# Seven more dummy products per layer on TensorE, in the pauses of the routing chain of a hybrid attention and mixture-of-experts backbone

## The reference, cut to what matters

```python
p_grp = softmax(h @ w_rg + b_rg)            # 4 groups
p_top, g_idx = top_k(p_grp, 1)              # one group
e_in = (h @ w_re + b_re)[group g_idx]       # 8 experts in it
l_top, e_loc = top_k(e_in, 2)               # two experts
w_tok = p_top * softmax(l_top)
...                                         # tokens sorted by expert, in blocks of 128 rows
yb = (silu(xblk @ w_gate[e]) * (xblk @ w_up[e])) @ w_down[e]
out = zeros.at[row_tok].add(yb * row_w)
```

## Time and profile before

| what | us |
|---|---|
| median of 3 executions (2642.61 to 2646.21) | 2644.64 |
| the profiled execution, whole | 2650.5 |
| its span from first to last instruction | 2648.7 |
| TensorE busy in it | 2452.0 (93%) |
| VectorE, ScalarE, GpSimd busy | 944.8, 662.6, 352.6 |

### The profile page before, as it was taken

One profiled execution on the slowest core, in us unless ns is written; L12 is line 12 of the kernel. 1 busy time (PEld: TensorE's weight loads), 2 busy tenths in 40 slices (PEclk: granted clock), 3 DMA queues, 4 the chain that ended last, 5 costly groups with the idle time before them and its releaser, 6 DMA issues.

```text
span 2648.7 us, 32996 instructions
## 1 busy us (share of the span) xinstructions
PE 2452.0 (93%) x12867; PEld 1556.2 (59%) x12867; DVE 944.8 (36%) x1791; ACT 662.6 (25%) x1242; POOL 352.6 (13%) x404
## 2 busy tenths in 40 slices
PE   7999999999999798999996999999999988999995
PEld 4768666788888633443332668667888733343332
DVE  3335466622225730000003635566334731111113
ACT  3231445632222200110111521456333200000000
POOL 1241000000112220010001531000011220010002
PEclk9999999999999889999998999999999889999998
DMA  8671001322214599999998471004433799999995
GB/s 283 205 269 49 7 1 45 78 61 70 64 56 167 216 387 422 427 422 425 427 427 326 165 245 48 7 1 98 113 96 109 294 374 424 427 421 424 427 427 198
DMA packets 218636, 604.66 MB, mean 228 GB/s; under 512 B 63360, under 2 KB 139552, under 8 KB 184944
## 3 DMA queue, kind: packets, MB, share of 16 engines
q1 hardware_dynamic: 190514, 526.80, 52.1%
q0 software_dynamic: 24512, 63.13, 6.8%
q10 hardware_dynamic: 3456, 12.58, 1.2%
HBM read 585.96 MB, written 38.16 MB: 236 GB/s over the span
## 4 chain that ended last, share of the span: by engine, by line
PE 71%; DMA 14%; DVE 7%; ACT 3%; issue 2%; SPq 1%; POOL 1%; DVEq 0%; ACTq 0%; POOLq 0%
PE slot L1239 23%; PE abank L778 18%; PE vbank L778 10%; DMA arena<-in_w_down_e 6%; DMA arena<-in_w_up_e 5%; PE slot L961 2%; PE vbank L995 1%; PE abank L878 1%; PE vbank L942 1%; DMA arena<-in_w_in 1%; PE slot L1022 1%; PE vbank L768 1%; PE slot L706 1%; PE vbank L1055 1%; DMA arena<-in_w_ada 1%
## 5 line engine op out<-in xcount | busy, mean ns | idle before, releaser
L1239 PE MATMUL slot<-arena 128*64 128x512 f32 (+2 forms) x3232 | 817.4, 613 | 66.6 <-DMA arena<-in_w_up_e 39.9
L1239 PEld LDWEIGHTS slot<-arena 128*64 128x64 f32 (+2 forms) x3232 | 296.1, 146 | 535.0 <-issue 527.2
L778 PE MATMUL abank<-round,round 128*128 128x512 f32 (+1 forms) x1792 | 492.7, 355 | 7.2 <-ACT arena L2275 2.1
L778 PEld LDWEIGHTS abank<-round,round 128*128 128x128 f32 x1792 | 318.7, 189 | 71.2 <-issue 15.9
L778 PE MATMUL abank<-hT_low,round 128*128 128x512 f32 (+1 forms) x896 | 318.1, 355 | 0.0
L778 PE MATMUL vbank<-round,round 128*128 128x512 f32 (+3 forms) x1248 | 289.9, 361 | 6.9 <-issue 5.8
L2110 DVE TENSOR_TENSOR arena<-slot,arena 128x512 f32<-128x512 f32 x76 | 52.6, 692 | 652.8 <-ACT arena L2515 378.8
L778 PEld LDWEIGHTS vbank<-round,round 128*128 128x128 f32 x1248 | 215.2, 189 | 41.8 <-issue 9.2
L778 PEld LDWEIGHTS abank<-hT_low,round 128*128 128x128 f32 x896 | 168.7, 188 | 23.9 <-issue 0.5
L1818 DVE TENSOR_TENSOR arena<-vbank,arena 128x512 f32<-128x512 f32 x72 | 43.4, 602 | 291.9 <-PE vbank L778 284.3
L2692 POOL TENSOR_TENSOR arena<-arena 128x512 f32<-128x512 f32 (+1 forms) x48 | 55.9, 1164 | 578.5 <-DVE arena L1818 578.5
(11 more groups left out here) (337 smaller groups left out, 2882.4 us busy)
## 6 DMA issues: line engine op xcount, KB each, us to landing
arena<-in_w_down_e SPq DMA_DIRECT2D x44, 2048.0 KB, 22.8
arena<-in_w_gate_e SPq DMA_DIRECT2D x40, 2048.0 KB, 25.0
arena<-in_w_up_e SPq DMA_DIRECT2D x40, 2048.0 KB, 29.8
arena<-in_w_up_e SPq DMA_DIRECT2D x48, 1024.0 KB, 13.0
arena<-in_w_gate_e SPq DMA_DIRECT2D x44, 1024.0 KB, 12.5
arena<-in_w_ada POOLq DMA_DIRECT2D x80, 512.0 KB, 4.9
arena<-in_w_down_e SPq DMA_DIRECT2D x40, 1024.0 KB, 29.9
arena<-in_w_in SPq DMA_DIRECT2D x48, 512.0 KB, 4.2
```

The lines of the kernel that those rows point to most:

```text
L778: last = pe.matmul(to, x, y, start=(k == 0 and q == 0), stop=(k == len(terms) - 1 and q == 2))
L1239: last = pe.matmul(to[at, cols], x[:, at], w[:, at_w, :], start=first, stop=final)
```

## The change

In each layer one dummy is added ahead of the router of the last tile, one after it, two ahead of the placement products, and three ahead of the first gathered rows. These are seven in each layer and fourteen in all. Nothing else changes; a line is added, so that lines of the new kernel from 1173 on stand one higher.

```diff
                     elif n == len(qt) - 1:
-                        keep_clock(spare, 1)
+                        keep_clock(spare, 2)
                     router(n)
-                keep_clock(spare, 2)
+                keep_clock(spare, 3)
 
                 pe.wait_ge(route_v, 3 * L + 1)
...
                 close(last, vgroups)
 
+                keep_clock(slot[0], 2)
                 ps = vec()
                 for k in range(2):
                     pe.wait_ge(route_p, 4 * L + k + 1)
...
-                keep_clock(slot[0], 2)
+                keep_clock(slot[0], 5)
                 xt_done, at_done = {}, {}
```

## The result

The changed kernel takes 2656.21 us (median of 17 executions, 2648.40 to 2661.72) against 2646.21 us for the kernel before (17 executions, 2642.22 to 2650.31). The ratio is 1.0036, with a 95% interval of 1.0029 to 1.0044: about 10 us slower. The forecast was 2645.5 us, range 2641.2 to 2650.0. The profiled execution after took 2659.0 us with a span of 2657.2 us, 8.5 us longer than that of before.

The account below looks back on a forecast made before the run. The prediction took the routing chain to bound the kernel until the weight stream takes over. Its terms, -1.2 us in layer 0 and +2.1 in layer 1, made +0.9, giving 2645.5 us from 2644.64, range 2641.2 to 2650.0.

Parts of the forecast that it names:

- What counts is what of it lies in a pause: Pricing step: fourteen dummies cost 12.0 us at full clock, 24.1 at half, but only work not hidden in pauses counts.
- B: Rival: the five dummies at the first rows run at half clock throughout, 8.6 us; 2650.4 us, chance 0.09.
- C: Rival: five dummies end in time, but the clock falls again during the rows' transposes and copies; 2649.9 us, chance 0.06.
- The row that the prediction set against C: Layer 1 before: the clock came back at 2135.3, right behind eight transposes of the first rows.
- The sum without this term: Net of all priced parts: -1.2 us in layer 0 and +2.1 in layer 1, together +0.9 us.
- One more ahead of the last router: Added dummy delays the last router's transposes, with no pause to hide it: +1.2 us layer 0, +0.9 layer 1.
- One more behind it: Three dummies after the last router run at full clock, hidden by VectorE's choosing: 0.1 us for both layers.
- rank and placement products wait for VectorE as before: Sign of a right forecast: dummies behind the last router and at the placement stay hidden, delaying neither product group.
- Two at the placement: Two dummies ahead of the placement products end before the second group may start: 0, at most 0.2 us.
- Five at the rows: Five dummies ahead of the first rows start at half clock, take 6.4 to 7.4 us: +0.6 layer 0, +2.0 layer 1.
- What comes back: Full clock behind the five dummies speeds rows' transposes and layer 0's first experts: 3.1 us layer 0, 0.9 layer 1.
- The test on the last router: Sign of a right forecast: the last router's transposes start about 1.6 us later against VectorE's line 1894.

Follow-up runs that it names:

- experiment 1: Kernel before with no dummy added but 56 idle semaphore increments in layer 1's expert phase: 2652.38 us, ratio 1.0026.
- experiment 2: Changed kernel with all fourteen dummies plus 200 idle increments, moving layer 1's loop by 256 in all: 2647.89 us, ratio 1.0000 against the kernel before.
- experiment 10: Changed kernel, no fillers, with TensorE's loop over spare expert blocks skipped by a condition: 2648.43 us, ratio 1.0010 against the kernel before.
- experiment 4: Kernel before with five dummies in place of two ahead of the first rows, plus 232 idle increments: 2646.70 us, ratio 1.0012.
- experiment 3: Kernel before with 256 idle increments in layer 1's expert phase and nothing else: 2646.24 us, ratio 1.0004.
- experiment 9: Kernel before with TensorE's loop over spare expert blocks skipped by a condition: 2646.05 us, ratio 1.0003.
- experiment 11: Kernel before with 28 idle increments in layer 1's expert phase and nothing else: 2653.42 us in one execution.
- experiment 12: Kernel before with 84 idle increments in layer 1's expert phase and nothing else: 2647.52 us in one execution.

## Why the prediction was wrong

**The step that failed** is the sentence on which the sum was built, "What counts is what of it lies in a pause." It takes it that an added instruction costs only where it runs. The prediction priced fourteen dummies in their pauses. Nowhere did it ask what the 56 instructions move behind them. The missing term is about +7 us: experiment 1 measures +6.8 us (+4.2 to +9.3), and the profile shows 5.75 us of it between the last experts and the mixing product. The loop's place makes up about 7 of the 10 us; the other 3 have no cause shown, and experiments 2 and 10 leave 2.3 and 3.0 us by their medians, with intervals that hold zero. No rival had this mechanism either, and B and C, whose times came nearest, had another cause: the five did not run at half throughout (experiment 4 and the profile after), and the clock was full at the first expert products of both layers. The row that the prediction set against C settles less than it says, as 3.78 us of dummies ran ahead of those eight transposes.

**The sum without this term** was +0.9 us (+0.8 before its parts are rounded), and experiment 2 measures 0.0 (-2.4 to +2.6). Point by point:

- *One more ahead of the last router, +2.1 us.* The profile after has the pair at 2.69 us against 1.49 in layer 0, and 3.33 against 1.82 in layer 1, where the transposes behind it win back 0.5 us (1.41 against 1.91). That is 1.2 and 1.0 us more, near the 1.2 and 0.9 forecast. In layer 0 that is luck in part: the pair was the shorter for running partly at full clock, and the transposes won nothing back (1.67 against 1.72), where the forecast had 1.7 for the dummy and 0.45 back. (By its own times, a start at 916.2 and the clock back at 916.8, it should have had three transposes at half and about 0.6 back.) Alone its time can't be told from nothing.
- *One more behind it, 0.1 us.* Mis-sized as an argument: "the router in front of them has just run at full clock" does not keep the clock up. The rank products were late by 1.6 us in both layers of the profile after, and in seven of ten layers over all traces with the three dummies, so the sign "rank and placement products wait for VectorE as before" failed for the rank products. The other bound that the prediction named, half clock and 2.4 us late, has as much right as the one taken. The lateness does not show in the time of experiment 2.
- *Two at the placement, 0.* Right: full clock, hidden, and the dummy behind them at 1.10 us instead of 2.05.
- *Five at the rows, 6.4 to 7.4 us long.* Right, 6.58 and 6.91 us. Layer 1 is late by 2 to 3 us against the +2.0 taken.
- *What comes back, 3.1 and 0.9 us.* Against the one profile before, the durations came back as forecast: 0.60 for 1.12, and 3.65 for 5.81. But that was one execution: in five of ten cases of experiments 1, 3, 9, 11 and 12 the first experts ran at full clock without any added dummy. Five dummies gave full clock in all eight cases (the profile after, experiments 2, 4 and 10), so they make sure of what otherwise came in half of the cases, and the 3.1 us hold for that one execution. What they are worth to the end can't be read apart from the rest.
- *The test on the last router* ("transposes start about 1.6 us later against VectorE's line") would have misled. In layer 0 of the profile after they started 5.4 us behind the start of that line (911.58 to 916.96) against 1.79 before. Only 1.2 us of that is the new dummy; 2.4 us come from the products ahead of it, which are unchanged and ran at half clock in this execution.

What stays open: why a loop is slow at one place of the stream and quick at others. The runs show where it is slow, that two steps of each turn take longer and one step of the first turn much longer, and that it is not the count of instructions. They don't show what in the chip does it. Also open is whether the changed kernel with the loop skipped (+0.1%, -0.01 to +0.21%) still loses some 3 us through its dummies; the runs can't tell that from nothing.

## What to carry to other kernels

When an edit adds instructions, look in both traces at what stands far behind it as well, above all at loops of branches close to the critical path: compare the turn time of each loop before believing that the added work costs the time. A control that moves the old kernel by the same number of idle instructions, and one that moves the new kernel on to another place, separate the two in two runs. And a filler product that is hidden only at full clock should be priced at half clock: here that is mostly what it got in seven of ten cases. The clock read off one profile is one draw: the kernel before showed both levels at the same products in other executions.

## What the runs showed of the hardware that was not expected

- A loop of ten turns without any work took 1.13 to 1.14 us a turn on TensorE's sequencer where it was moved by 0, 28, 84 or 256 instructions, and 1.59 to 1.60 us where it was moved by 56, by dummies and by fillers alike. The kernel lost 6.8 us (+4.2 to +9.3) by that.
- The first turn is uneven too, with nothing in it either. In layer 1 it took 2.0 us in the kernel before, 4.1 in the changed one and in experiment 1, and 1.0 to 3.5 where the loop was quick; in layer 0 it took 5.7 us before and 5.8 after. In the changed kernel 3.1 of the 4.1 us lie in the step to the branch that closes the turn, the same step that is slow in its later turns.
- The granted clock fell to 0.50 over 2120 to 2122 although TensorE had been busy without a pause over the stretch before it, at 0.98, with the router's products of 36 columns. The same six records took 2.82 us or 4.52 us in neighbouring layers of one execution.
